# Attention keys of the second mixer: stored whole and split after the reload, with ScalarE and SyncE work moved around them

## The chip, the cores and the metric

The kernel runs on one core of a Trainium2 chip. The metric is the time of one execution in microseconds on the device. Engines are named as in the profile: PE is TensorE (PEld its weight loads), ACT is ScalarE, DVE is VectorE, POOL is GpSimd, SP is SyncE, which here does nothing but issue DMAs.

## The reference, cut to what matters

Two transformer blocks in a row work on 256 tokens of width 1024 in float32, and the second has 16 more rows of "meta tokens" in front, so 272 key rows. The second block's mixer projects its input and runs two attentions, a windowed one with grouped heads (16 query heads over 4 key heads) and a differential one (8 heads, each with two query and key parts):

```
q, k = rope(q), rope(k)
s_band = einsum(q, k_window) * scale; p = softmax([s_band, s_meta, sink])      # windowed
p = softmax(einsum(q, k) * scale + key_bias); a = p[0] - lam * p[1]; o = a @ v # differential
merged = 0.5 * (1 + tanh(..)) gates of both, @ w_out
```

## The kernel before, in words

**Products from two parts.** A float32 number is held as a high part in fp32r and a low part, `low = x - high`, also fp32r. ACT makes the high part (a copy that rounds), DVE or POOL the low part (a subtraction), and PE adds the products of the parts.

**Weights.** They come in blobs of 1 MB, one DMA each into a `raw` buffer (L748). ACT makes `whi` (L862), DVE makes `wlo` (L1859), and PE multiplies. In the second mixer three buffers take turns; `m2` counts its blobs from 0. A load waits until the blob three before it is split; a `whi` waits until the blob three before it is used up.

**Slots.** A blob is multiplied in two halves. After half `part` of blob `m2` PE runs `slot(q)` with `q = 2 * m2 + part`; ACT, DVE, and after the change POOL, have a loop over the same `q`, in which the order of their work is written out by hand, and no engine leaves its order. In the slots q = 22 to 53 PE makes the scores of one attention unit each, U = 0 to 31 (0 to 15 windowed, 16 to 31 differential). Unit U goes through: scores on PE in slot 22 + U (L1755), maximum on DVE and exponentials on ACT (L1165) in 23 + U, DVE's reciprocal (L2075) and for windowed units ACT's scaling (L1197) also in 23 + U, transposes on PE in slot 24 + U (L1689), values on PE in slot 25 + U.

**What the blobs hold.** Blobs 0 to 4 give keys, blobs `QUERIES` give queries, blobs `VALUES` give values. Key and query blobs are rotated: ACT (with DVE) moves the result from PSUM to `kraw`, SP's `swap_halves` copies it with swapped partition halves to `kswap` (two DMAs, L786 and L787), DVE multiplies both by the tables in `turn` and adds them into `kswap` (L2347 to L2349 for keys, L2337 to L2340 for queries). `kraw` and `kswap` have two buffers, by `m2 % 2`.

**Keys before.** `keys_high` (ACT, L1104) makes the high part in `knat`, POOL the low part (L1357), `store_keys` (SP, L794 to L798) writes both to DRAM as `key_parts`, 544 KB a blob. From there SP loads one chunk at a time to `kB`, two DMAs of 272 KB (L805): chunks 0 and 1 behind the loads of blobs 12 and 13, for the windowed units, and one for each two differential units.

**Queries.** `queries_high` (ACT, L1112) makes high parts twice, POOL the low part `ql` (L1364), SP moves it (L826).

**Values.** `values_out` (ACT, L1122) moves the values of a blob from PSUM to `kraw`, PE transposes them at the head of the slot in `VALUES_AT` (L1726), and `values_in` (ACT, L1138) brings them back in the next slot. PE waits in that slot for `values_out`.

## Time and profile before

| what | value |
| --- | --- |
| median of 3 runs | 876.76 us (876.65 to 877.49) |
| profiled execution | 876.87 us, of it 875.1 us span from first to last instruction |
| PE busy | 862.2 us, 99% of the span |
| PE weight load busy | 737.9 us, 84% |
| DVE, ACT, POOL busy | 629.0 (72%), 468.0 (53%), 73.7 (8%) |
| granted PE clock | 0.999 of full speed |

Time outside the span is 1.8 us. Slot 0 begins at about 396 us of the span. "Idle before" in a row names what ended the idle time.

### The profile page before, as it was taken

How to read it: one execution, taken by the hardware profiler on the slowest of the kernel's cores; microseconds unless marked ns; L12 is line 12 of the kernel's file. 1: busy time of each engine (PE TensorE's matmuls, PEld its weight loads, DVE VectorE, ACT ScalarE, POOL GpSimd, SP SyncE). 2: the span in 40 equal slices, each digit the busy share in tenths (PEclk: the TensorE clock that was granted, in tenths of full speed). 3: DMA queues.
4: the chain of work that ended last, by engine and by line, in shares of the span. 5: the costliest groups of instructions: out<-in, count | busy, mean ns of one | idle time of the engine just before them, and what ended most of it. 6: DMA issues, size and time to landing. Idle time of an engine off the chain costs nothing.

```text
span 875.1 us, 13099 instructions
## 1 busy us (share of the span) xinstructions
PE 862.2 (99%) x4820; PEld 737.9 (84%) x4820; DVE 629.0 (72%) x985; ACT 468.0 (53%) x756; POOL 73.7 (8%) x96
## 2 busy tenths in 40 slices
PE   8999999999999999999999999999999999999997
PEld 6887788888888888889889888788888888888886
DVE  5867677766876666668778887888766876666665
ACT  6546534434644444444566887676653654444443
POOL 1000000000200000002322010133300100000000
PEclk9999999999999999999999999999999999999999
DMA  9955344554565555352798443755474365455531
GB/s 331 400 212 192 116 169 149 192 188 149 186 241 191 192 192 192 144 192 86 259 274 288 136 157 117 246 192 172 169 269 173 122 225 190 177 198 188 189 143 48
DMA packets 31774, 167.21 MB, mean 191 GB/s; under 512 B 4128, under 2 KB 5920, under 8 KB 14320
## 3 DMA queue, kind: packets, MB, share of 16 engines
q1 hardware_dynamic: 28992, 159.17, 51.8%
q10 hardware_dynamic: 2736, 7.42, 2.4%
q8 instruction: 29, 0.48, 0.2%
q14 instruction: 17, 0.14, 0.0%
HBM read 157.02 MB, written 3.83 MB: 184 GB/s over the span
## 4 chain that ended last, share of the span: by engine, by line
PE 86%; DVE 6%; ACT 3%; DMA 1%; issue 1%; POOL 1%; SPq 0%; ACTq 0%; DVEq 0%
PE ps L522 16%; PE ps L524 16%; PE ps L523 16%; PE ps L688 8%; PE ps L673 8%; PE ps L692 4%; PE ps L669 4%; PE ps L701 2%; DVE wlo L1859 2%; ACT whi L862 1%; PE ps L557 1%; PE ps L1755 1%; DMA kswap<-kraw 1%; PE ps L703 1%; PE ps L1713 1%
## 5 line engine op out<-in xcount | busy, mean ns | idle before, releaser
L1859 DVE TENSOR_TENSOR wlo<-raw,whi 128x2048 fp32r<-128x2048 f32 x134 | 307.4, 2295 | 146.3 <-ACT whi L862 145.9
L862 ACT ACTIVATE whi<-raw 128x2048 fp32r<-128x2048 f32 x134 | 256.2, 1913 | 180.0 <-PE ps L524 109.0
L522 PE MATMUL ps<-whi,xT 128*128 128x512 f32 x192 | 76.8, 400 | 0.0
L524 PE MATMUL ps<-whi,xT 128*128 128x512 f32 x192 | 75.0, 391 | 0.0
L523 PE MATMUL ps<-wlo,xT 128*128 128x512 f32 x192 | 74.8, 390 | 0.0
L1326 POOL TENSOR_TENSOR stat<-stat,cst 128x1 f32<-128x1 f32 x10 | 11.9, 1200 | 490.0 <-DVE stat L1879 261.0
L522 PE MATMUL ps<-whi,fT_h 128*128 128x512 f32 x128 | 50.2, 392 | 0.0
L523 PE MATMUL ps<-wlo,fT_h 128*128 128x512 f32 x128 | 49.8, 389 | 0.0
L524 PE MATMUL ps<-whi,fT_l 128*128 128x512 f32 x128 | 49.8, 389 | 0.0
L522 PE MATMUL ps<-x_all,whi 128*128 128x272 f32 x160 | 46.5, 291 | 1.6 <-DVE wlo L1859 1.5
L523 PE MATMUL ps<-x_all,whi 128*128 128x272 f32 x160 | 46.1, 288 | 0.0
L524 PE MATMUL ps<-x_all,wlo 128*128 128x272 f32 x160 | 46.1, 288 | 0.0
L1165 ACT ACTIVATE sc<-sc,usoft 128x272 f32<-128x272 f32 x64 | 32.7, 512 | 22.7 <-DVE usoft L2067 18.7
L524 PEld LDWEIGHTS ps<-whi,xT 128*128 128x128 f32 x192 | 36.0, 188 | 7.8
L522 PEld LDWEIGHTS ps<-whi,xT 128*128 128x128 f32 x192 | 36.1, 188 | 7.4
L523 PEld LDWEIGHTS ps<-wlo,xT 128*128 128x128 f32 x192 | 36.1, 188 | 7.0
L673 PE MATMUL ps<-x_all,whi 128*128 128x512 f32 x176 | 42.0, 391 | 0.0
L688 PE MATMUL ps<-x_all,whi 128*128 128x512 f32 x160 | 38.0, 390 | 0.0
L522 PE MATMUL ps<-whi,x_all 128*128 128x512 f32 x96 | 38.0, 396 | 0.0
L524 PE MATMUL ps<-whi,x_all 128*128 128x512 f32 x96 | 37.7, 393 | 0.0
L673 PEld LDWEIGHTS ps<-x_all,whi 128*128 128x128 f32 x176 | 32.3, 188 | 6.3
L523 PE MATMUL ps<-wlo,x_all 128*128 128x512 f32 x96 | 37.6, 391 | 0.0
(349 smaller groups left out, 1886.9 us busy)
## 6 DMA issues: line engine op xcount, KB each, us to landing
raw<-weights SPq DMA_DIRECT2D x134, 1024.0 KB, 4.8
kB<-key_parts SPq DMA_DIRECT2D x20, 272.0 KB, 3.5
kswap<-kraw SPq DMA_DIRECT2D x26, 136.0 KB, 2.5
key_parts<-knat SPq DMA_DIRECT2D x4, 544.0 KB, 7.3
cst<-consts SPq DMA_DIRECT2D x1, 1371.0 KB, 13.3
raw<-weights SPq DMA_DIRECT2D x4, 256.0 KB, 5.1
raw<-weights SPq DMA_DIRECT2D x2, 512.0 KB, 6.7
gate_a<-gain_rows ACTq DMA_DIRECT2D x2, 512.0 KB, 7.9
```

The source lines that it names most:

```text
L522: pe.matmul(o, lh, rh, start=first, stop=False)
L523: pe.matmul(o, lh, rl, start=False, stop=False)
L524: return pe.matmul(o, ll, rh, start=False, stop=last)
L669: pe.matmul(ps[:, bank0 + j, 0:TOK], vl[:, k, j * P:(j + 1) * P], x[:, 0, k, :], start=k == 0, stop=False, skip_group_check=True)
L673: m = pe.matmul(ps[:, bank0 + j, :], vh[:, k, j * P:(j + 1) * P], x[:, :, k, :], start=False, stop=k == KC - 1, skip_group_check=True)
L688: pe.matmul(ps[:, bank0 + j, :], vh[:, k, j * P:(j + 1) * P], x[:, :, k, :], start=k == 0, stop=False)
L692: m = pe.matmul(ps[:, bank0 + j, 0:TOK], vl[:, k, j * P:(j + 1) * P], x[:, 0, k, :], start=False, stop=k == KC - 1)
L701: pe.matmul(ps[:, bank + j, :], vh[:, k, j * P:(j + 1) * P], x2[:, :, k, :], start=k == 0, stop=False)
L862: act.activation(whi[s][:], raw[s][:], ACT.Copy).then_inc(split_hi, 1)
L1165: ins = act.activation(scores(U, u), scores(U, u), ACT.Exp, bias=st[:, 2, u:u + 1], accum_out=st[:, 4, u:u + 1])
L1326: pool.tensor_tensor(st[:, 3:4], st[:, 2:3], c("neghalf")[:, 0:1], ALU.pow).then_inc(rstd_ok, 1)
L1859: dve.tensor_tensor(wlo[s][:], raw[s][:], whi[s][:], ALU.subtract).then_inc(split_lo, 1)
```

## The change

Keys are stored as they come from the rotation, unsplit (272 KB a blob), straight from `kswap`. A chunk is loaded back to a new buffer `ktwo` (two of them), and only then ACT makes its high part and POOL its low part in `kB`. That takes place in ten steps e = 0 to 9, in the slots of the new table `KEYS_AT`. `queries_high` moves from ahead of the exponentials to the end of its slot, the DMAs of the gate rows `gate_s` move from ACT to SP, and blob 11 now holds queries and blob 12 values (before the other way round).

```diff
-QUERIES = (6, 7, 9, 10, 12, 13, 15, 17)
+QUERIES = (6, 7, 9, 10, 11, 13, 15, 17)
-VALUES = (5, 8, 11, 14, 16)
+VALUES = (5, 8, 12, 14, 16)
-VALUES_AT = {12: 0, 18: 1, 24: 2, 30: 3, 34: 4}
+VALUES_AT = {12: 0, 18: 1, 26: 2, 30: 3, 34: 4}
+KEYS_AT = {17: 0, 19: 1, 32: 2, 38: 3, 40: 4, 42: 5, 44: 6, 46: 7, 48: 8, 50: 9}
+def stored(i):
+    return 16 * (i // 2 + 1) + (0 if i % 2 else 32)
...
@@ SP: swap_halves
-                if swaps_before(m2):
-                    sp.wait_ge(kt_ok, max(SWAPPED.index(m) for m in SWAPPED if m < m2 and m % 2 == b) + 1)
+                last = max((m for m in SWAPPED if m < m2 and m % 2 == b), default=None)
+                if last in QUERIES:
+                    sp.wait_ge(kt_ok, QUERIES.index(last) + 1)
+                elif last is not None:
+                    sp.wait_ge(kd_out[b], stored(last))
@@ SP: store_keys
-                sp.wait_ge(kt_ok, i + 1)
-                parts = knat[i % 2][:].bitcast(F32)
+                sp.wait_ge(rot_ok, i + 1)
+                v = kswap[i % 2]
                 if i:
-                    sp.dma_start(kd[i], parts).then_inc(kd_out[i % 2], 16)
+                    sp.dma_start(kd[i], v[:]).then_inc(kd_out[i % 2], 16)
@@ SP: load_keys, in the iterations 12 to 15 and 22 to 27 of the load loop
+                i, cc = (0, e) if e < 2 else (e // 2, e % 2)
+                if e == 0:
+                    sp.wait_ge(kd_out[0], stored(4))
+                    sp.wait_ge(kd_out[1], stored(3))
+                if e >= 2:
+                    sp.wait_ge(kb_lo, e - 1)
+                for u in range(2):
+                    v = kd[i, u::2, cc].unsqueeze(1).to_broadcast([DH, 2, KEYS])
+                    sp.dma_start(ktwo[e % 2][:, u, :], v).then_inc(ktwo_in[e % 2], 16)
...
+                if m == 22:
+                    sp.wait_ge(u_sc, S_UNITS)
+                    for t in range(NT):
+                        sp.dma_start(gate_s[:, t, :], grow[5].partition_broadcast(P)).then_inc(bias_in[2], 16)
@@ ACT
+            def keys_high(e):
+                act.wait_ge(ktwo_in[e % 2], 32 * (e // 2 + 1))
+                if e >= 2:
+                    act.wait_ge(u_sc, sets_read(e))
+                act.activation(kB[e % 2][:, :, 0, :], ktwo[e % 2][:], ACT.Copy).then_inc(kb_hi, 1)
...
-                if q in (4, 6, 8, 10, 12):
-                    keys_high(q // 2 - 2)
-                if q % 2 == 1 and (q - 5) // 2 in QUERIES:
-                    queries_high((q - 5) // 2)
...
-                if q == 38:
-                    act.wait_ge(u_sc, S_UNITS)
-                    bias_rows(2, gate_s)
+                if q % 2 == 1 and (q - 5) // 2 in QUERIES:
+                    queries_high((q - 5) // 2)
+                if q in KEYS_AT:
+                    keys_high(KEYS_AT[q])
@@ POOL, now in the same loop over q, in ACT's order
+            def keys_rest(e):
+                pool.wait_ge(kb_hi, e + 1)
+                pool.tensor_tensor(kB[e % 2][:, :, 1, :], ktwo[e % 2][:], kB[e % 2][:, :, 0, :],
+                                   ALU.subtract).then_inc(kb_lo, 1)
@@ PE
-                        pe.wait_ge(kb_in[key_slot(U)], keys_loaded(U))
+                        pe.wait_ge(kb_lo, key_set(U) + 1)
```

**First place.** ACT in the slots q = 16 to 20, before (L1112 is `queries_high`, L1122 `values_out`, L862 a `whi`, L1138 `values_in`):

```order
L862 ACTIVATE whi_56<-raw_55 128x2048
L1112 ACTIVATE qs_135<-kswap_119 128x512
L1112 ACTIVATE qs_136<-kswap_119 128x512
L1122 ACTIVATE kraw_117<-ps 128x544
L862 ACTIVATE whi_59<-raw_58 128x2048
L1134 ACTIVATE vb_meta<-ps 16x256
L1138 ACTIVATE vb<-ps,stat 128x256 x2
L1112 ACTIVATE qs_135<-kswap_120 128x512
```

and in the changed kernel (lines 5 higher; L1109 is the new `keys_high`):

```order
L867 ACTIVATE whi_56<-raw_55 128x2048
L1117 ACTIVATE qs_135<-kswap_119 128x512
L1117 ACTIVATE qs_136<-kswap_119 128x512
L1109 ACTIVATE kB_123<-ktwo_121 128x2x272
L1127 ACTIVATE kraw_117<-ps 128x544
L867 ACTIVATE whi_59<-raw_58 128x2048
L1139 ACTIVATE vb_meta<-ps 16x256
L1143 ACTIVATE vb<-ps,stat 128x256 x2
```

`keys_high(0)`, which waits for a DMA, now stands ahead of `values_out(1)`, the values of blob 8.

**Second place.** ACT in the slots q = 25 and 26, before (L1165 exponentials, L1176 and L1181 small copies, L1197 scaling, L1096 `queries_low`):

```order
L1138 ACTIVATE vb<-ps,stat 128x256 x2
L1112 ACTIVATE qs_135<-kswap_119 128x512
L1112 ACTIVATE qs_136<-kswap_119 128x512
L1165 ACTIVATE sc_142,usoft<-sc_142,usoft 128x272 x2
L1168 ACTIVATE usoft<-usoft 128x2
L1176 ACTIVATE pmT<-ps 48x128
L1181 ACTIVATE sT_h<-ps 128x128
L1197 ACTIVATE sc_142<-sc_142,usoft 128x272 x2
L1096 ACTIVATE kraw_117<-ps 128x2x256
```

and in the changed kernel:

```order
L1166 ACTIVATE sc_142,usoft<-sc_142,usoft 128x272 x2
L1169 ACTIVATE usoft<-usoft 128x2
L1177 ACTIVATE pmT<-ps 48x128
L1182 ACTIVATE sT_h<-ps 128x128
L1198 ACTIVATE sc_142<-sc_142,usoft 128x272 x2
L1117 ACTIVATE qs_135<-kswap_119 128x512
L1117 ACTIVATE qs_136<-kswap_119 128x512
L1127 ACTIVATE kraw_117<-ps 128x544
```

The last row, `values_out(2)`, now stands here, behind the scaling and behind `queries_high` of blob 10; before, it stood in slot 24, right behind the scaling of unit 0.

**Third place.** DVE in slot q = 24, before (L2337 to L2340 rotate the queries of blob 10, L2074 and L2075 end unit 1's row sums):

```order
L2065 TENSOR_TENSOR usoft<-usoft,negsink 128x2
L2337 TENSOR_TENSOR kraw_117<-kraw_117,turn 128x2x256
L2338 TENSOR_TENSOR kswap_119<-kswap_119,turn 128x2x256
L2340 TENSOR_TENSOR kswap_119<-kraw_117,kswap_119 128x2x256
L2074 TENSOR_TENSOR usoft<-usoft 128x2
L2075 RECIPROCAL usoft<-usoft 128x2
```

and in the changed kernel (12 lines higher):

```order
L2077 TENSOR_TENSOR usoft<-usoft,negsink 128x2
L2341 TENSOR_TENSOR kraw_118<-ps,kraw_118 128x2x256
L2349 TENSOR_TENSOR kraw_117<-kraw_117,turn 128x2x256
L2350 TENSOR_TENSOR kswap_119<-kswap_119,turn 128x2x256
L2352 TENSOR_TENSOR kswap_119<-kraw_117,kswap_119 128x2x256
L2086 TENSOR_TENSOR usoft<-usoft 128x2
L2087 RECIPROCAL usoft<-usoft 128x2
```

The first step of blob 11's queries, `queries_raw` (L2341), now stands ahead of the rotation; it waits for ACT's `queries_low` of the same slot.

## Rows read from the trace of the kernel before

**Rows 1.** Waits of PE over the whole span: us in total, times, longest:

```profile
PE ps L701 <- ACT vs L1138: 1.7, 1, 1.7
PE ps L522 <- DVE wlo L1859: 1.5, 1, 1.5
...
PE ps L1689 <- DVE sT_l L2407: 0.8, 1, 0.8
PE ps L1726 <- ACT kraw L1122: 0.6, 1, 0.6
```

**Rows 2.** Timeline of DVE in the key stage: start, us, what, idle before:

```profile
415.92 0.72 DVE L2349 TENSOR_TENSOR kswap<-kraw,kswap 128x544 f32<-128x544 f32 x1
...
423.78 0.73 DVE L2347 TENSOR_TENSOR kraw<-kraw,turn 128x544 f32<-128x544 f32 x1 [0.28 <-DMA kswap<-kraw]
424.42 1.90 DVE L2348 TENSOR_TENSOR kswap<-kswap,turn 128x544 f32<-128x544 f32 x1
...
437.59 0.72 DVE L2347 TENSOR_TENSOR kraw<-kraw,turn 128x544 f32<-128x544 f32 x1 [2.92 <-DMA kswap<-kraw]
...
439.63 2.29 DVE L1859 TENSOR_TENSOR wlo<-raw,whi 128x2048 fp32r<-128x2048 f32 x1
```

**Rows 3.** Timeline of POOL, the low part of key blob 1:

```profile
424.32 1.41 POOL L1357 TENSOR_TENSOR knat<-kswap,knat 128x544 fp32r<-128x544 f32 x1 [5.54 <-ACT knat L1104]
```

**Rows 4.** Timeline of SP, the DMA issues named in the text:

```profile
418.81 0.50 SPq L796 DMA_DIRECT2D key_parts<-knat  x1
...
441.94 0.33 SPq L748 DMA_DIRECT2D raw<-weights  x1
443.13 0.33 SPq L794 DMA_DIRECT2D key_parts<-knat  x1
...
452.76 1.58 SPq L805 DMA_DIRECT2D kB<-key_parts  x2
```

**Rows 5.** Issue to landing of the three weight loads (L748) issued from 405 to 423:

```profile
DMA to landing us min/median/max: 4.8/5.0/5.1
```

**Rows 6.** The same of the three stores of key blob 0 (418 to 421):

```profile
DMA to landing us min/median/max: 2.1/2.4/2.6
```

**Rows 7.** The same of L786, the first half of swaps, from 403 to 422:

```profile
DMA to landing us min/median/max: 2.2/2.3/2.3
```

**Rows 8.** The same of the two key loads (L805) issued at 452.8 and 453.8:

```profile
DMA to landing us min/median/max: 6.8/7.8/8.7
```

**Rows 9.** Timeline of PE: blobs 7 and 9, value transposes, unit transposes:

```profile
443.64 2.08 PE L701 MATMUL ps<-x_all,whi 128*128 128x512 f32 x8 [1.70 <-ACT vs L1138]
...
455.32 2.01 PE L701 MATMUL ps<-x_all,whi 128*128 128x512 f32 x8
...
458.13 0.38 PE L1726 MATMUL ps<-cst,kraw 128*128 128x128 f32 x2
...
481.72 0.60 PE L1689 MATMUL ps<-cst,sc 128*128 128x128 f32 x4
...
486.58 0.66 PE L1689 MATMUL ps<-cst,sc 128*128 128x128 f32 x4
```

**Rows 10.** Timeline of ACT: value copies, scalings and query parts named in the text:

```profile
457.14 0.60 ACT L1122 ACTIVATE kraw<-ps 128x544 f32<-128x544 f32 x1
...
475.69 0.94 ACT L1197 ACTIVATE sc<-sc,usoft 128x272 f32<-128x272 f32 x2 [2.36 <-DVE usoft L2075]
...
479.11 0.94 ACT L1197 ACTIVATE sc<-sc,usoft 128x272 f32<-128x272 f32 x2 [0.20 <-DVE usoft L2075]
...
482.74 1.14 ACT L1112 ACTIVATE qs<-kswap 128x512 fp32r<-128x512 f32 x2
...
485.59 0.94 ACT L1197 ACTIVATE sc<-sc,usoft 128x272 f32<-128x272 f32 x2 [0.30 <-DVE usoft L2075]
```

**Rows 11.** Timeline of DVE, the low part of blob 14, in slot 25:

```profile
481.89 2.29 DVE L1859 TENSOR_TENSOR wlo<-raw,whi 128x2048 fp32r<-128x2048 f32 x1 [1.11 <-ACT whi L862]
```

**Rows 12.** Timeline of ACT in slot 38, behind the issue of the gate rows:

```profile
551.36 1.92 ACT L862 ACTIVATE whi<-raw 128x2048 fp32r<-128x2048 f32 x1 [0.54 <-issue]
```

More of the change, by code:

```diff
@@ L143, in query_of, with key_set, sets_read @@
     return U // S_UNITS * 4 + cc // 2
-def key_slot(U):
+def key_set(U):
     cc, _ = unit_place(U)
-    return cc // 4 if U < S_UNITS else cc % 2
-def keys_loaded(U):
-    cc, _ = unit_place(U)
-    return 32 if U < S_UNITS else 32 + 32 * (cc // 2 + 1)
+    return cc // 4 if U < S_UNITS else 2 + cc
+def sets_read(e):
+    return 0 if e < 2 else 8 if e == 2 else 2 * e + 10
+def stored(i):
+    return 16 * (i // 2 + 1) + (0 if i % 2 else 32)
 def slot_of(n):
@@ L299, in build @@
         kswap = [new("kswap0", [P, 2, KEYS]), new("kswap1", [P, 2, KEYS])]
-        keys_at = top[0]
-        knat = [new("knat0", [P, 2, 2, KEYS], F32R), new("knat1", [P, 2, 2, KEYS], F32R)]
-        top[0] = keys_at
-        kB = [new("kB0", [P, 4, KEYS]), new("kB1", [P, 4, KEYS])]
+        ktwo = [new("ktwo0", [P, 2, KEYS]), new("ktwo1", [P, 2, KEYS])]
+        kB = [new("kB0", [P, 2, 2, KEYS], F32R), new("kB1", [P, 2, 2, KEYS], F32R)]
         vs_meta = new("vs_meta", [P, S_KV * DH])
         o_junk = new("o_junk", [P, P])
-        rrow2 = at("rrow2", [P, TOK], F32, top[0])
-        ql = [new("ql0", [P, 2, TOK], F32R)]
+        rrow2 = new("rrow2", [P, TOK])
         assert top[0] <= 3 * BLOB
@@ L435, in build @@
         kd_out = [sem("kd_out0"), sem("kd_out1")]
-        kb_in = [sem("kb_in0"), sem("kb_in1")]
+        ktwo_in = [sem("ktwo_in0"), sem("ktwo_in1")]
+        kb_hi = sem("kb_hi")
+        kb_lo = sem("kb_lo")
         q_in = [sem(f"q_in{j}") for j in range(len(QUERIES))]
@@ L1096, in queries_low @@
                 act.activation(kraw[b][:, :, 0:TOK], ps[:, bank:bank + 2, TOK:2 * TOK], ACT.Copy).then_inc(ql_ok, 1)
-            def keys_high(i):
-                act.wait_ge(rot_ok, i + 1)
-                if i >= 2:
-                    act.wait_ge(kd_out[i % 2], 16 * (i // 2) + (0 if i % 2 else 32))
-                act.activation(knat[i % 2][:, :, 0], kswap[i % 2][:], ACT.Copy).then_inc(rot_hi, 1)
+            def keys_high(e):
[3 more added lines that the diff above has]
+                act.activation(kB[e % 2][:, :, 0, :], ktwo[e % 2][:], ACT.Copy).then_inc(kb_hi, 1)
             def queries_high(m2):
                 i = QUERIES.index(m2)
-                act.wait_ge(rot_ok, 5 + i + 1)
+                act.wait_ge(rot_ok, SWAPPED.index(m2) + 1)
                 j = QUERY_PLACE[i]
@@ L1353, in _, with queries_rest @@
             pool.memset(pmT[:], 0.0).then_inc(zero2, 1)
-            for i in range(5):
+            def queries_rest(m2):
+                i = QUERIES.index(m2)
+                j = QUERY_PLACE[i]
                 pool.wait_ge(rot_hi, i + 1)
-                pool.tensor_tensor(knat[i % 2][:, :, 1], kswap[i % 2][:], knat[i % 2][:, :, 0],
-                                   ALU.subtract).then_inc(kt_ok, 1)
-            for i, m2 in enumerate(QUERIES):
-                pool.wait_ge(rot_hi, 5 + i + 1)
                 if i >= 2:
                     pool.wait_ge(q_in[QUERY_PLACE[i - 2]], 32)
-                j = QUERY_PLACE[i]
                 pool.tensor_tensor(ql[i % 2][:], kswap[m2 % 2][:, :, 0:TOK],
@@ L1366, in _ @@
                                    ALU.subtract).then_inc(kt_ok, 1)
-            for U in range(S_UNITS, UNITS):
-                pool.wait_ge(d_o, U - S_UNITS + 1)
-                st = ostat[:, U % 3]
-                link(pool, "pool", rsqrt(st[:, 2:3], st[:, 1:2], st[:, 0:1], 1.0 / P))
-                pool.tensor_scalar(o_tok[U % 3][:], o_tok[U % 3][:], st[:, 2:3], None, ALU.mult).then_inc(d_n, 1)
+            def keys_rest(e):
+                pool.wait_ge(kb_hi, e + 1)
+                pool.tensor_tensor(kB[e % 2][:, :, 1, :], ktwo[e % 2][:], kB[e % 2][:, :, 0, :],
+                                   ALU.subtract).then_inc(kb_lo, 1)
+            for q in range(2 * OUT2):
+                if q % 2 == 1 and (q - 5) // 2 in QUERIES:
+                    queries_rest((q - 5) // 2)
+                if q in KEYS_AT:
+                    keys_rest(KEYS_AT[q])
+                U = q - U0 - 3
+                if S_UNITS <= U < UNITS:
+                    pool.wait_ge(d_o, U - S_UNITS + 1)
+                    st = ostat[:, U % 3]
+                    link(pool, "pool", rsqrt(st[:, 2:3], st[:, 1:2], st[:, 0:1], 1.0 / P))
+                    pool.tensor_scalar(o_tok[U % 3][:], o_tok[U % 3][:], st[:, 2:3], None, ALU.mult).then_inc(d_n, 1)
             for t in range(NT):
@@ L1755, in slot @@
                             m = pe.matmul(ps[:, 4 + u, 0:KEYS], qT[u][:, cc, t * P:(t + 1) * P],
-                                          kT[:, 2 * u + v, 0:KEYS].bitcast(F32R), start=v == 0, stop=v == 1)
+                                          kT[:, u, v, :], start=v == 0, stop=v == 1)
                     m.then_inc(u_sc, 1)
```

40 lines of the change are left out of this document (14 added, 26 removed).

## The prediction

> **What bounds the kernel now.** I read the page first: PE is busy 99% of the span at its full clock, so apart from its start and end the kernel is as long as PE's own work plus PE's waits. The changed kernel gives PE the same products and transposes. What the change can win or lose is therefore PE's waits in the second mixer, and the list of PE's waits shows all that there is to win [rows 1]: 1.5 us for the low part of blob 5, 1.7 for `vs`, the values of blob 5, 0.6 for `values_out(3)`, 0.8 for `sT_l` in slot 40; 4.6 us in all. What there is to lose has no such limit. So I followed the timelines of DVE, SP and ACT through slots 4 to 40 and asked at each wait of PE what is late next. Times below are on the clock of the profiled execution (span 875.1 us, with 1.8 us around it 876.9; the median of the runs, 876.76, is 0.1 lower).
>
> **Key stage, slots 4 to 15.** Removed: five ACT copies, five POOL subtractions, half of the bytes of the stores. Added: a swap into `kswap` must now wait until the store that reads it has *landed*, where before it waited for POOL.
>
> Rotation of key blob 0 ends at 415.92 + 0.72 = 416.6 [rows 2]. Its stores went out at 418.8, behind ACT and POOL [rows 4]; now at 416.7. Three issues take some 1.2 us and the last lands 2.1 later [rows 6], at 420.0; the swap's second half leaves 0.6 behind the first and lands after another 2.4 (the first half took 2.3 [rows 7]): 423.0, against 423.75 before, when DVE woke up [rows 2]. The rotation then takes 2.0 (437.59 to 439.63), without the 1.2 us which one of its steps lost, 1.90 for 0.72, while POOL worked from 424.32 to 425.73 [rows 2, 3]. With 2.3 for the low part, blob 5 is ready at 427.35, when PE comes: the wait of 1.5 goes.
>
> For blobs 3 and 4 the new wait costs what the removed work gives. Their stores stand behind a weight load of 1 MB, which lands 4.8 to 5.1 after its issue [rows 5]. For blob 4: weight load out at 428.3, landed at 433.3, the store 0.7 behind it (a guess: half of the 1.4 that the transfer of the 544 KB appears to take), swap out at 434.1 and 434.7, landed at 437.0, against 437.6 before [rows 2]. 2.0 + 2.3 later, at 441.4 to 441.8, blob 7 is ready, against 441.9. `vs` is ready before that, since `keys_high(4)` no longer stands in front of it on ACT. PE begins blob 7 at about 441.65 instead of 443.64 [rows 9]: **-2.0 us** so far, with a short wait left.
>
> **Slot 18, `keys_high(0)` ahead of `values_out(1)`.** This is the first place of the order. PE does 455.32 - 443.64 = 11.7 us for blobs 7 and 8 and 2.8 for the first half of blob 9 [rows 9], so it stands at the transposes of blob 8's values at 458.13 - 2.0 = 456.1. It needs `values_out(1)`, which before ran at 457.14 [rows 10], and now waits on ACT behind `keys_high(0)`, thus for the landing T of the first key chunk. T from SP's order: weight load 10 can leave when blob 7 is split, 441.65 (before 441.94 [rows 4]); it lands 5.0 later and the store of key blob 4 0.7 behind it, 447.3. Only then may the swap of blob 6 leave (new wait), and SP with it; 1.2 for its two issues, weight load 11 at 448.6, the swap of blob 7, weight load 12 at 450.7, the key chunk at 451.3 and 451.9 (before from 452.76 [rows 4]). Ahead of the chunk stand two weight loads and a swap. From below: load 11 lands 5.0 after 448.6, and of those 5.0 some 2.3 are there for a small DMA as well [rows 7], so load 12 takes 2.7 more, swap and chunk some 0.5 each: 457.3. From above: the chunk lands as late after its issue as before, 6.8 and 8.7 [rows 8], 458.1 and 460.6. I take T = 458.5. The copy and `values_out(1)` take 0.6 each [rows 10]: PE goes on at 459.8 against 458.13, **+1.65** on before, which swallows the 2.0 (a wait of 3.7 us). Bounds -0.1 to +3.6 (T from 456.7 to 460.5); no wait at all needs T below 454.8. The scores of slot 22 wait for `kb_lo` of this chunk, ready at 461, and are no problem.
>
> **Slots 24 to 26, second and third place.** From here on I use before's times and count only what differs, since all follows PE. Blob 11 is queries, so DVE in slot 24 has `queries_raw(11)` ahead of the rotation of blob 10. It waits for `queries_low(11)` on ACT, which waits behind `queries_high(9)`, now behind the scaling of unit 0. That began at 475.69 and took 0.9 [rows 10]; DVE's sums in front of it had met POOL's low part of blob 9, which now comes later, so it begins some 1.1 earlier (what POOL cost DVE in slot 6) and ends at 475.5: 475.5 + 1.1 + 0.6 = 477.1. `queries_raw` 0.7, rotation 2.0 with 0.2 lost to POOL's low part of blob 9, sums 0.3: 480.3; scaling 0.9 [rows 10]: 481.3. PE comes to the transposes of unit 1 at 480.9 (before 481.72 [rows 9], 0.4 less for the shorter blob, 0.6 less for the value transposes that went to slot 26, 0.2 more for the values blob now in hand). So it starts them at 481.35: a wait of 0.5.
>
> Behind the scaling ACT makes the high part of blob 14 (1.9), 483.1; DVE the low part (2.3), 485.45 (before at 481.89 [rows 11]); sums and scaling of unit 2 end at 486.75 (before 485.59 + 0.94 = 486.5 [rows 10], and PE took it at 486.58 [rows 9]). Now `queries_high(10)` follows (1.14 [rows 10]) and then `values_out(2)` (0.6): 488.3. PE is at the transposes of blob 12's values at 486.2, waits 2.1, and starts unit 2 after 0.57 more (the six value transposes) at 488.9 instead of 486.58: **+2.3**. Bounds: +0.9 if the sums of unit 1 and of unit 2 come 0.7 earlier each; +3.1 if POOL's subtraction (1.4 [rows 3]) holds up DVE's `queries_raw` too.
>
> One row bears on that last bound. In slot 6 the DVE step from `kswap` and `turn`, both in SBUF, ran 1.90 and ended 0.6 after POOL, as if it had begun when POOL ended [rows 2, 3]. The Trainium skill (SBUF — State Buffer, "Who interferes with whom") says that DVE with two inputs in SBUF and a POOL operation that reads SBUF exclude each other for a whole instruction, whoever comes first. The trace agrees, 1.90 for 0.72. By that rule `queries_raw`, which has one input in PSUM, isn't held, as I assumed above; were it held, the sum would be 0.8 higher.
>
> **Later slots.** `values_out(3)` in slot 30 loses what stood in front of it (`queries_high(12)` in slot 29 is gone): PE's 0.6 goes, **-0.65** with its start. In slot 38 the gate rows' issue cost ACT 0.54 [rows 12]; in its place stands `keys_high(3)`, 0.6: nothing. In slot 39 `queries_high(17)` comes later and POOL's part falls on DVE's sums, scaling and `sT_l`: the wait of 0.8 in slot 40 stays, **+0.2** (bounds -0.8 to +0.5). The seven key steps in slots 38 to 50 cost ACT 0.6 each and may each hold DVE 1.1. I cost them at nothing: PE waits nowhere after slot 40 [rows 1], and ACT (53% busy) and DVE (72%) run ahead of it there. Without that cover each would cost up to 1.7, 12 us in all. The loads of the chunks leave two slots or more before their step; SP's wait for the last windowed unit (slot 37) stands before weight load 23, needed in slot 42.
>
> **Sum.** -2.0 + 3.65 (slot 18, that is +1.65 net) + 2.3 - 0.65 + 0.2 = **+3.5 us**: 880.3 us on the median. Its own range by the bounds is 877.5 to 883.5.
>
> **Rivals.** *The chunk is in time* (chance 0.10). The chunk's DMAs are issued behind two weight loads but may overtake them: before, the first of the two key loads took 6.8 and the second 8.7 though issued one after the other [rows 8], so they are not in step. Both must land, by 454.8, 3 us after the issue. Against it: the second took 8.7. Then slot 18 costs nothing and the sum is -2.0 + 2.3 - 0.65 + 0.2 = -0.15: 876.6. The Trainium skill (DMA: Bandwidth & Descriptors, "Queues, rings and completion order") says that the DMAs of one issuing engine need not complete in order, which would make this more likely than a strict queue does; the trace shows it for halves of pairs alone.
>
> *Only slot 18 costs* (0.14): ACT is a microsecond or two earlier in slot 26 than I have it, PE finds `values_out(2)` ready; -2.0 + 3.65 - 0.65 + 0.2 = +1.2: 878.0.
>
> *ACT never holds PE* (0.12), the other side: ACT is far enough ahead at both value copies. The place is ACT's order ahead of L1127, the price of it is both waits; it decides when `values_out(1)` is done by 456.1 and `values_out(2)` by 486.2. Then the relief of the key stage stays, slots 30 and 40 give their waits back as well: -2.0 - 0.65 - 0.8 = -3.5: 873.3. For it: the key traffic is halved, and a weight load that stands alone takes 5.0, not more.
>
> *Traffic gets worse* (0.04): small stores and swaps each waiting for the one before, T at 464: 885.
>
> *As forecast* 0.60.
>
> **Numbers.** About 0.2% (1.75 us) is what a measurement of this kernel can tell from no change, so "same" is 875.0 to 878.5. Faster: all of the third rival and a part of the first, 0.16. Same: most of the first, half of the second and the low edge of the forecast, 0.18. Slower 0.66. The range 876.0 to 883.6 holds the forecast, the first two rivals and leaves out the third.
>
> **What would show it.** Key stage: no wait of PE for blob 5, blob 7 begun near 441.7, swaps issued right after a store's landing. Slot 18: PE waits 2 to 5 us for `kraw` of ACT (L1127), and ACT before that for the DMA `ktwo`. Slot 26: PE waits about 2 us for `kraw` again. Slot 30: no wait. Slots 41 to 53: none. The prediction is wrong above all if ACT's wait for `ktwo` in slot 17 is under 1 us, or if a key step of the later slots holds DVE long enough to stop PE.

## Result and the profile after

The changed kernel took **884.4 us** (median of 6 runs, 883.4 to 886.7), the kernel before 876.7 on the same chip: a ratio of 1.0089, interval 1.0076 to 1.0103. Run once more beside other experiments it took 884.5 (1.0102, 1.0084 to 1.0119). The forecast was 880.3, slower, with a range up to 883.6: the sign and the places were right, the sum was 4.1 us short.

One profiled execution, that of the run with the shorter delay below (c2), ran at a granted clock of 0.65 throughout and took 1222.8 us; it is used nowhere.

The first profiled execution took 886.7, 2.3 above the median. The rows here are those of a second one, of 884.5 (span 882.7 against 875.1 before), unless the text says "first". PE's waits over the whole span, in the columns of [rows 1]:

```profile
PE ps L1738 <- ACT kraw L1127: 7.2, 2, 5.4
PE ps L708 <- DVE wlo L1871: 2.3, 2, 1.2
...
PE ps L1753 <- issue: 0.3, 1, 0.3
PE ps L529 <- DVE wlo L1871: 0.2, 1, 0.2
```

Of the four waits of [rows 1] three are gone, that of blob 5 nearly; in their place stand two waits for the landing of a store in the key stage (blobs 6 and 7) and two for a value copy (slots 18 and 26). The timeline of PE there:

```profile
442.16 1.21 PE L708 MATMUL ps<-x_all,whi 128*128 128x512 f32 x4 [1.19 <-DVE wlo L1871]
...
462.21 0.69 PE L1738 MATMUL ps<-cst,kraw 128*128 128x128 f32 x2 [5.36 <-ACT kraw L1127]
...
463.40 3.11 PE L708 MATMUL ps<-x_all,whi 128*128 128x512 f32 x8
...
493.52 0.44 PE L1738 MATMUL ps<-cst,kraw 128*128 128x128 f32 x2 [1.86 <-ACT kraw L1127]
```

The first row answers to 443.64 in [rows 9], the second to 458.13: PE comes 1.5 us earlier into blob 7, and 4.1 later to the end of its wait in slot 18. The timeline of ACT says why, in both slots:

```profile
460.99 0.66 ACT L1109 ACTIVATE kB<-ktwo 128x544 fp32r<-128x544 f32 x1 [6.66 <-DMA ktwo<-key_parts]
461.55 0.60 ACT L1127 ACTIVATE kraw<-ps 128x544 f32<-128x544 f32 x1
...
490.99 0.94 ACT L1198 ACTIVATE sc<-sc,usoft 128x272 f32<-128x272 f32 x2 [1.21 <-DVE usoft L2087]
491.83 1.13 ACT L1117 ACTIVATE qs<-kswap 128x512 fp32r<-128x512 f32 x2
492.87 0.60 ACT L1127 ACTIVATE kraw<-ps 128x544 f32<-128x544 f32 x1
```

In slot 17 ACT waited 6.7 us for the DMA of `keys_high(0)` (L1109), with `values_out(1)` (L1127) behind it. In slot 26 `values_out(2)` stands behind the scaling and `queries_high(10)`: PE stood there from 491.66, the scaling ended 0.3 later, and the copies of both took the rest of the wait. Issues of SP, and the time from issue to landing of the two loads of chunk 0:

```profile
442.51 0.43 SPq L804 DMA_DIRECT2D key_parts<-kswap  x1
448.18 0.47 SPq L796 DMA_DIRECT2D kswap<-kraw  x1
...
452.01 1.59 SPq L820 DMA_DIRECT2D ktwo<-key_parts  x2
```

```profile
DMA to landing us min/median/max: 7.0/7.5/7.9
```

The swap of blob 6 left when the store had landed. The two loads of the chunk, issued at 452.0 and 453.0, landed at 459.0 and 461.0.

**What I had not looked for** is in the third PE row. The same eight matmuls, right behind the value transposes, took 3.11 us here and 2.08 before:

```profile
458.71 2.08 PE L701 MATMUL ps<-x_all,whi 128*128 128x512 f32 x8
```

Windows of the first profiled execution over two stretches, one from the end of the wait in slot 18 on, one behind the wait in slot 26 (us, busy time and count of PE, PEld, DVE, ACT, POOL, then PE's granted clock, DMA share, GB/s):

```profile
460.69:467.52 6.83, 5.64 (x19) 4.70 (x20) 2.29 (x1) 5.49 (x9) 3.15 (x3) 0.50 0.25 92
494.83:498.24 3.41, 3.41 (x22) 2.69 (x20) 2.34 (x5) 0.83 (x6) 0.45 (x1) 0.50 0.39 154
```

TensorE ran at 1.2 GHz instead of 2.4 in both. In the second execution the stretch began at 458.8, inside the wait, and ended at 465.6, and none followed slot 26. Before, the clock was at 2.4 GHz from 9.5 us of the span to its last 2 us.

The price of a stretch can be read behind slot 26. Nine profiles (these two and seven of the experiments) have that wait. From its end to the scores of slot 27 PE took 7.0 us in the three in which no stretch follows, and 8.5 to 8.6 us in the six in which one does.

Where the 7.6 us between the two profiled executions (875.1 and 882.7) lie, read from the start of PE's score matmuls, which every slot from 22 to 53 has once:

| place | forecast | measured |
|---|---|---|
| key stage, start of blob 7 | -2.0 | -1.5 |
| slot 18, value transposes 458.13 to 462.21 | +3.65 | +5.6 |
| slots 18 to 22, clock at half | 0 | +1.4 |
| slots 24 to 26 | +2.3 | +2.1 |
| slot 30 | -0.65 | -0.8 |
| slot 40 | +0.2 | -1.0 |
| slots 44 to 53 | 0 | +1.8 |
| sum | +3.5 | +7.6 |

The last place, slots 44 to 53, in the scores of slots 44 and 53, before and after:

```profile
576.82 0.75 PE L1755 MATMUL ps<-kB,qd 128*128 128x272 f32 x4
...
616.51 0.75 PE L1755 MATMUL ps<-kB,qd 128*128 128x272 f32 x4
```

```profile
582.67 0.75 PE L1767 MATMUL ps<-kB,qd 128*128 128x272 f32 x4
...
624.13 0.75 PE L1767 MATMUL ps<-kB,qd 128*128 128x272 f32 x4
```

39.7 us became 41.5. I call this the late stretch below.

### The profile page after: what moved, and what is told of

The parts are those of the page before. It is cut to its first block, busy times and chain, and to the rows that moved or that the text cites. A ratio compares the mean times of both kernels' runs of the same rounds, so it can differ in the third digit from the quotient of the medians.

```text
span 884.9 us, 13113 instructions
## 1 busy us (share of the span) xinstructions
PE 866.8 (98%) x4820; PEld 740.4 (84%) x4820; DVE 625.8 (71%) x985; ACT 468.9 (53%) x761; POOL 78.4 (9%) x101
## 4 chain that ended last, share of the span: by engine, by line
PE 92%; DMA 3%; DVE 2%; ACT 1%; SPq 1%; issue 1%; DVEq 0%; ACTq 0%
PE ps L529 18%; PE ps L531 17%; PE ps L530 17%; PE ps L695 8%; PE ps L680 7%; PE ps L699 4%; PE ps L676 4%; PE ps L1767 2%; PE ps L708 2%; DMA key_parts<-kswap 1%; PE ps L564 1%; PE ps L1701 1%; PE ps L710 1%; DMA ktwo<-key_parts 1%; PE ps L1725 1%; PE ps L1720 1%
## 5 line engine op out<-in xcount | busy, mean ns | idle before, releaser
L1328 POOL TENSOR_TENSOR stat<-stat,cst 128x1 f32<-128x1 f32 x10 | 9.9, 1003 | 489.4 <-DVE stat L1891 260.4
```

## Experiments

The kernels ran in sets on different chips, each beside the kernel before, whose median there was 875.8 to 877.0 us. The ratio in brackets is to that median, with its interval. So times of different sets can't be told apart below 1 us; there the profiles have to decide.

**The chunk one slot later.**

```
-KEYS_AT = {17: 0, 19: 1, ...
+KEYS_AT = {18: 0, 20: 1, ...
```

> The changed kernel with the high parts of key chunks 0 and 1 made in slots 18 and 20 instead of 17 and 19, so that `values_out(1)` stands ahead of the wait for the first chunk. Theory A (the wait of 5.4 us in slot 18 costs itself and, through TensorE's granted clock at 0.5 for 6.8 us behind it, some 2 us more): PE finds `values_out(1)` ready, no stretch at 0.5 begins near 460, and the time falls by 6.5 to 7.5 us to about 877.4. Theory B (the wait alone counts, the time at the lower clock is hidden under what PE would have waited for anyway): 884.4 - 5.4 = 879.0. Theory C (ACT and SP are held by the landing of the chunk wherever the step stands, so the wait comes back one or two slots later at a weight blob): 882 or more.

Measured: 883.7 us (ratio to before 1.0074, 1.0062 to 1.0087). C was right. `values_out(1)` was in time, and the wait stood one step further on ACT, at `values_in(1)`, which frees the PSUM pair (timeline of PE, then of ACT):

```profile
463.53 2.90 PE L708 MATMUL ps<-x_all,whi 128*128 128x512 f32 x6 [3.90 <-ACT vb L1143]
```

```profile
459.95 0.66 ACT L1109 ACTIVATE kB<-ktwo 128x544 fp32r<-128x544 f32 x1 [5.91 <-DMA ktwo<-key_parts]
460.51 1.89 ACT L867 ACTIVATE whi<-raw 128x2048 fp32r<-128x2048 f32 x1
462.31 0.36 ACT L1139 ACTIVATE vb_meta<-ps 16x256 f32<-16x256 f32 x1
462.58 0.80 ACT L1143 ACTIVATE vb<-ps,stat 128x256 f32<-128x256 f32 x2
```

From the landing of the chunk to PE's release it is now 3.6 us instead of 1.2, so that the wait of 5.4 us became only 3.9, although PE came 2.8 later to it and the chunk landed 1.0 earlier. The median fell by 0.7, which is within the two intervals.

**The chunk behind all of it.**

```
-KEYS_AT = {17: 0, 19: 1, ...
+KEYS_AT = {20: 0, 21: 1, ...
```

> The changed kernel with the high parts of key chunks 0 and 1 in slots 20 and 21, behind both `values_out(1)` (slot 18) and `values_in(1)` (slot 19). Theory A (the chunk's landing near 460.6 costs only because values of blob 8 stand behind it on ACT; with slot 18 alone passed by, the wait moved from 5.4 us at L1127 to 3.9 us at L1143): both waits gone, and the time at a granted clock of 0.5 that begins behind them too: 884.4 - 5.4 - 1.5 to 2 = 877.2. Theory B (ACT has no place before slot 22 at which the chunk can be taken without holding PE; the wait moves to a weight blob or to the scores of slot 22): 881 or more.

Measured: 877.3 (1.0016, 1.0003 to 1.0028), 7.1 below the changed kernel, or 6.4 by the two ratios. A was right: the wait was 5.4, and the rest went with it. The chunk landed no earlier (461.3); now nothing stood behind it on ACT that PE was waiting for. Of PE's waits for ACT one was left, slot 26:

```profile
PE ps L1738 <- ACT kraw L1127: 1.9, 1, 1.9
```

**The chunk's DMA ahead of the others.** The loads of chunk 0 are issued behind the store of blob 4, ahead of the swap of blob 6; ACT's place stays slot 17.

```
                 if 6 <= m < 11:
                     store_keys(m - 6)
+                if m == 10:
+                    load_keys(0)
-                if 12 <= m < 16:
+                if 13 <= m < 16:
```

> The changed kernel with one thing moved: SP issues the loads of key chunk 0 right behind the store of key blob 4, when this has landed, and ahead of the swap of blob 6, instead of behind two weight loads and the swaps of blobs 6 and 7. ACT's step stays in slot 17. Theory A (the landing at 460.6 is late because the chunk was issued at 451.7 and 452.7 behind two weight loads, and the landing, not ACT's place alone, makes the wait): issued at 448 to 449, ahead of the loads issued later, it lands by 453 to 455, ACT does not wait into slot 18, and the time is that of key steps in slots 20 and 21, 877.3. Theory B (the chunk's load takes 7 to 8 us whenever it is issued, since weight loads issued behind it share the queues): landing near 456.5, a wait of PE of about 1.5 us in slot 18, 878.5 to 880. Theory C (the swap of blob 6, later by 1.2 us, is what becomes late): a wait of 1 us or more for the queries of blob 6 or for `values_out(1)` behind them.

Measured: 881.0 (1.0049, 1.0033 to 1.0064). The landing was as A said and far below B's 7 to 8 us:

```profile
DMA to landing us min/median/max: 2.5/2.7/2.8
```

The same two loads of 136 KB take 2.5 and 2.8 us with no weight load on its way, and 7.0 and 7.9 behind two weight loads of 1 MB and a swap. PE did not wait in slot 18. But the gain was half. What SP issued behind the chunk was later (the next weight load by 0.7, its landing by 1.8), and PE waited in four new places besides slot 26 (L1740):

```profile
PE ps L1740 <- ACT kraw L1129: 1.9, 1, 1.9
PE ps L1703 <- ACT sc L1200: 1.1, 1, 1.1
PE ps L1769 <- DVE usoft L2079: 0.5, 1, 0.5
PE ps L708 <- ACT vb L1145: 0.3, 1, 0.3
...
PE ps L708 <- DVE kraw L2343: 0.3, 1, 0.3
```

**Queries ahead of the exponentials again.** `queries_high` goes back to where it stood before, in all its slots.

```
+                if q % 2 == 1 and (q - 5) // 2 in QUERIES:
+                    queries_high((q - 5) // 2)
                 if q == 14:
...
-                if q % 2 == 1 and (q - 5) // 2 in QUERIES:
-                    queries_high((q - 5) // 2)
                 if q in KEYS_AT:
```

> The changed kernel with `queries_high` back ahead of the exponentials of its slot, and nothing else undone. Theory A (in slot 26 `values_out(2)` comes late because `queries_high(10)` stands between the scaling of unit 2 and it; the 1.85 us of PE's wait also bring a stretch of 3.4 us at a granted clock of 0.5, which costs about 1.6 more): both go, 884.4 - 3.4 = 881.0. Theory B (the wait alone): 882.6. Theory C (the wait of slot 26 comes from the scaling of unit 2 and the high part of the weight blob, and `queries_high` in front of the exponentials costs the units what it gives the values): 884.4 or more.

Measured: 885.1 (1.0099, 1.0084 to 1.0113). A and B are refuted, C was right: the wait of slot 26 stayed at 1.9 and a wait of 0.6 for `sT_l` came back in slot 40. The 1.1 us of `queries_high(10)` in front of `values_out(2)` were gone, but the scaling ended at 492.4, and PE stood at the value transposes from 491.1. The scaling was late because its row sum on DVE was. DVE's step here, and in the changed kernel:

```profile
490.02 1.25 DVE L2086 TENSOR_TENSOR usoft<-usoft 128x2 f32<-128x2 f32 x1
```

```profile
490.60 0.15 DVE L2086 TENSOR_TENSOR usoft<-usoft 128x2 f32<-128x2 f32 x1
```

With `queries_high(10)` earlier, POOL's low part of the same queries ran beside DVE's sums, from 488.90 to 491.25; in the changed kernel it began at 493.04, behind them. So the place of `queries_high(10)` costs about 1.1 us on either side of the scaling: as a copy behind it, or by POOL ahead of it.

**Blobs 11 and 12 as before.**

```
-QUERIES = (6, 7, 9, 10, 11, 13, 15, 17)
+QUERIES = (6, 7, 9, 10, 12, 13, 15, 17)
-VALUES_AT = {12: 0, 18: 1, 26: 2, 30: 3, 34: 4}
+VALUES_AT = {12: 0, 18: 1, 24: 2, 30: 3, 34: 4}
```

(`VALUES` and `TAKERS` go back with them.)

> The changed kernel with blobs 11 and 12 as before (11 values, 12 queries, `values_out(2)` in slot 24), all else as changed. Theory A (the order of the blobs costs PE its 1.85 us in slot 26, because DVE has the raw queries of blob 11 to make in slot 24 and ACT's scaling of unit 2 comes late; it gives back 0.65 in slot 30 and 1.0 in slot 40): 884.4 - 1.85 + 1.65 = 884.2, or 883 with a share of the clock. Theory B (`queries_high` behind the exponentials costs the 1.85 in whatever blob order): the wait stands in slot 24 or 26 again and slots 30 and 40 get their waits back, 886.

Measured: 883.3 (1.0079, 1.0062 to 1.0097). No wait in slot 24 or 26, none in slots 30 and 40 either. The order of the blobs, with the slot that it gives to `values_out(2)`, is the cause in slot 26, and undoing it gives nothing back elsewhere. The median is 1.1 us lower, which is within the intervals; between the scores of slots 22 and 30 PE took 38.4 us instead of 40.5 in the profiled executions. Together with the edit before (next run, of the same set as e5) it is clear of noise:

> Both edits: key chunks 0 and 1 in slots 20 and 21, blobs 11 and 12 as before. Theory A: the sum of the two single edits, 877.2 - 0.2 = 877.0, with what the late slots lose (1.8 us) still in it. Theory B (they are two covers of one lateness of ACT and DVE, so that the second edit gives nothing or less than alone): 877.2 to 879.

Measured: **875.4** (0.9990, 0.9981 to 0.9998): 1.9 below e5, which is the wait of slot 26, and 9 below the changed kernel. The granted clock is 1.0 up to the last 2 us, and these are PE's waits from 340 us on:

```profile
PE ps L708 <- DVE wlo L1871: 2.6, 2, 1.4
PE ps L1753 <- issue: 0.4, 1, 0.4
```

**Is the lower clock the wait's doing?** The kernel before, with copies of the unit matrix on ACT ahead of `values_out(1)` (the edit in short):

```
                 if i == 1:
+                    for o in (sT_h, qd[0], qd[1]):
+                        act.activation(o, unit matrix, ACT.Copy)
```

> The kernel before, with three copies of the unit matrix over 2048 columns (1.8 us each) put into ACT ahead of `values_out(1)` in slot 18; they write where nothing stands yet and change no result. PE had 0.4 us of margin there, so it should wait 5.4 - 0.4 = 5.0 us. Theory A (a wait of such length is itself followed by a stretch at a granted clock of 0.5, whoever causes it): such a stretch of some 3.4 to 6.8 us begins within 1 us behind the wait, and the time is 876 + 5.0 + 1.5 to 2 = 882.5 to 883. Theory B (the lower clock in the changed kernel comes from something else in it): clock 1.0 throughout, and 881.0 at most.

Measured: 882.3 (1.0068, 1.0054 to 1.0081); its profiled execution is the fastest of the six, 879.8, and the others took 881.9 to 883.2. The wait was 3.3 us in it, not 5.0: the copies began at 454.1, as soon as blob 8 was through, 2.8 us before PE stood at the transposes. The timeline of PE:

```profile
460.14 0.44 PE L1730 MATMUL ps<-cst,kraw 128*128 128x128 f32 x2 [3.31 <-ACT kraw L1126]
...
460.86 3.57 PE L701 MATMUL ps<-x_all,whi 128*128 128x512 f32 x8
```

The clock was 0.5 from 460.7 to 464.1, and eight matmuls took 3.57 instead of 2.08 (at 458.71): 1.5 us on top of the wait. B is refuted; the old kernel shows the same when PE is made to wait. With a shorter delay:

> As the run before, with one copy over 2048 columns and one over 512, 2.3 us: a wait of PE of 1.9 us in slot 18, as long as that in slot 26 of the changed kernel. In four profiles with a wait of 1.9 us in slot 26, three had a stretch of 3.4 us at 0.5 behind it and two had none; the waits of 1.1 to 1.7 us in the key stage never had one. Theory A: 876 + 1.9 = 877.9 without a stretch, 879.3 with one, so that single runs spread by 1.4 us. Theory B (a wait of under 2 us costs itself only): 877.9 and no stretch.

Measured: 876.3 (0.9998, 0.9987 to 1.0008), the median of executions of 875.4 to 878.0. The time doesn't show the delay; a delay of 2.3 us fits into the 2.8 us of room that the longer one had, but no usable profile shows that it did. So this run says nothing on the clock behind a short wait. (The count in its expectation is wrong: of the seven profiles with a wait of 1.9 us in slot 26 taken up to then, five had a stretch behind it and two had none.)

The changed kernel once more:

> The changed kernel once more, unchanged. Over its six times so far those with a mean clock of 0.998 were 883.4 and 883.6 us, with 0.996 884.1 and 884.7, with 0.994 884.7 and 886.7. Theory A (each stretch of 3.4 us at 0.5 costs about 1 us and comes and goes between executions): the same steps again, 1.0 to 1.3 us per 0.002 of mean clock, median 884.4. Theory B (the spread has another cause): no relation between clock and time.

Measured: 884.5. All eleven executions of the changed kernel, by the mean clock of the span:

| mean clock | us |
|---|---|
| 0.997 to 0.998 | 883.1, 883.4, 883.6 |
| 0.996 | 883.7, 884.1, 884.5, 884.7 |
| 0.993 to 0.994 | 884.7, 885.9, 886.2, 886.7 |

The means are 883.4, 884.3 and 885.9. The time follows the clock as A says, 0.9 and 1.6 us a step. That is a relation, not an intervention, but the eight matmuls at either level, and the 7.0 against 8.5 to 8.6 us behind slot 26, give such a price too.

**The late stretch.** Orders of the key steps and cuts of their halves, with a table of all at the end. First, POOL's normalisation ahead of `keys_rest`:

```
-                if q in KEYS_AT:
-                    keys_rest(KEYS_AT[q])
                 U = q - U0 - 3
                 if S_UNITS <= U < UNITS:
                     ...
+                if q in KEYS_AT:
+                    keys_rest(KEYS_AT[q])
```

> The changed kernel with POOL's normalisation of `o_tok` ahead of `keys_rest` in a slot that has both (slots 42 to 50). Theory A (PE loses some 1.8 us in slots 44 to 51 because `keys_rest` of 1.4 us stands ahead of the normalisation that PE's transpose of `o_tok` needs): 884.4 - 1.8 = 882.6. Theory B (the normalisation is late because DVE holds it up while it runs, 2.1 to 2.6 us instead of 0.6, whatever stands ahead of it): no change, 884.4.

Measured: 886.0 (1.0110, 1.0095 to 1.0124), 1.6 more on the median, which the intervals don't tell from nothing, but the late stretch took 42.4 instead of 41.5; neither theory had that. Together with the two first edits:

> The three edits together: key chunks 0 and 1 in slots 18 and 20, `queries_high` ahead of the exponentials, the normalisation ahead of `keys_rest`. Theory A (each loss is local and the clock's share goes with its wait): 884.4 - 7.0 - 3.4 - 1.8 = 872.2, faster than the kernel before by 0.5%. Theory B (waits alone, clock and order on POOL worth nothing): 884.4 - 5.4 - 1.85 = 877.1, as before. Theory C (a wait that goes in slot 18 comes back in part further on): 878 or more.

Measured: 887.9 (1.0119, 1.0104 to 1.0133). C, and worse. Of three repairs drawn from the trace alone none is measurably better than the changed kernel by itself (-0.7, +0.7 and +1.6 on the medians), and the three together are 3.5 slower. `keys_high` at the head of the slot for q from 38 on:

> The changed kernel with the key steps of slots 38 to 50 (ACT's copy) at the head of their slot, ahead of the exponentials, so that POOL's subtraction is through before the unit's `o_tok` comes. Theory A (PE's loss of 1.8 us in slots 42 to 53 comes from the collision of POOL's two steps with the low part of the weight blob on DVE, and an earlier `keys_rest` takes it away): 882.6. With the normalisation first the loss had grown by about 1 us instead, since the subtraction then ran into DVE's next steps. Theory B (any subtraction of 1.4 us on POOL in these slots holds DVE for as long, wherever it stands): 884.4, or more if the exponentials come late by 0.6.

Measured: 889.2 (1.0138, 1.0121 to 1.0155). The late stretch gained 0.3, but PE waited 2.1 us for `sT_l` in slot 40, and a third stretch at clock 0.5, of 3.4 us, began 0.9 behind that wait.

Then the halves of the step, cut to 16 of 272 columns on the kernel of 875.4:

> Key chunks 0 and 1 in slots 20 and 21 and the blobs as before, and POOL's subtraction for chunks 4 to 9 over 16 of 272 columns only, so that the low part of these keys is left out for the rest (what remains there is that of an earlier chunk). Theory A (the 1.85 us that slots 44 to 53 lose is POOL's 1.4 us per key step, which pushes the normalisation of `o_tok` into the low part of the weight blob): 875.4 - 1.7 = 873.7. Theory B (it is ACT's copy of 0.6 us in these slots that makes the unit's exponentials late): 875.4.

Measured: 875.1 (0.9986, 0.9976 to 0.9996). A is refuted: with most of POOL's subtraction gone the late stretch is as long, 41.4.

> Key chunks 0 and 1 in slots 20 and 21, the blobs as before, and for chunks 4 to 9 both ACT's copy and POOL's subtraction over 16 of 272 columns only: the split of the other columns is left out for the rest. With the subtraction alone cut it was 875.1, and the late slots took as long as before the cut. Theory A (ACT's copy of 0.64 makes the loss): copy of 0.2 us, the loss falls to a third or less, 875.2 - 1.2 to 1.8 = 873.6. Theory B (the loss is in neither, but in the loads of the chunks or in where PE stands): 875.1.

Measured: 873.7 (0.9972, 0.9963 to 0.9981), late stretch 39.8. A was right for ACT's copy on top of the subtraction; the copy cut alone was not run, so whether the subtraction would cost anything by itself in these slots isn't shown. The timeline of ACT and of DVE in slot 44, before:

```profile
577.76 0.34 ACT L1204 ACTIVATE dT_h<-ps,subgain 128x128 fp32r<-128x128 f32 x1
578.01 1.90 ACT L862 ACTIVATE whi<-raw 128x2048 fp32r<-128x2048 f32 x1
```

```profile
579.24 0.28 DVE L2067 TENSOR_SCALAR usoft<-usoft 128x2 f32<-128x2 f32 x1
579.94 2.29 DVE L1859 TENSOR_TENSOR wlo<-raw,whi 128x2048 fp32r<-128x2048 f32 x1 [0.43 <-ACT whi L862]
```

and in the changed kernel, with POOL last:

```profile
584.18 0.64 ACT L1109 ACTIVATE kB<-ktwo 128x544 fp32r<-128x544 f32 x1
584.73 1.90 ACT L867 ACTIVATE whi<-raw 128x2048 fp32r<-128x2048 f32 x1
```

```profile
585.61 0.69 DVE L2079 TENSOR_SCALAR usoft<-usoft 128x2 f32<-128x2 f32 x1
586.66 2.30 DVE L1871 TENSOR_TENSOR wlo<-raw,whi 128x2048 fp32r<-128x2048 f32 x1 [0.36 <-ACT whi L867]
```

```profile
584.91 1.36 POOL L1371 TENSOR_TENSOR kB<-ktwo,kB 128x544 fp32r<-128x544 f32 x1 [2.88 <-ACT kB L1109]
...
587.30 2.14 POOL L1384 TENSOR_SCALAR o_tok<-o_tok,ostat 128x128 f32<-128x128 f32 x1
```

`whi` starts 1.2 us behind the scores before (576.82) and 2.1 after (582.67); DVE's `wlo` is 0.9 later behind it, and the copies that PE needs in the next slot stand behind `wlo`; none of PE's waits there is longer than 0.3. ACT is idle for 1.6 us and more in the odd slots, but not in front of `whi`.

So the steps into the odd slots, where ACT has no weight blob, with POOL's normalisation first in this run and the ones after it:

```
-... 40: 4, 42: 5, 44: 6, 46: 7, 48: 8, 50: 9}
+... 40: 4, 41: 5, 43: 6, 45: 7, 47: 8, 49: 9}
```

> Key chunks 0 and 1 in slots 20 and 21 and the blobs as before (875.4 us), and in addition the steps of key chunks 5 to 9 in slots 41, 43, 45, 47, 49 instead of 42 to 50, POOL's normalisation of `o_tok` ahead of `keys_rest`. Theory A (the late slots lose 1.85 us because in even slots ACT's copy of 0.64 stands ahead of the high part of the weight blob, and so DVE's low part and the sums and `puT` behind it are late; in odd slots ACT has no weight blob and is idle for 1.6 to 2.7 us): slots 44 to 53 take 39.7 us again, 875.4 - 1.5 to 1.8 = 873.7. Theory B (any key step in these slots costs PE its 0.3 to 0.4 us, as did the steps at the head of the slot and with the normalisation first): 875.4.

Measured: 875.3 (0.9992, 0.9983 to 1.0001), late stretch 41.2: B. And with POOL's half cut there:

> The kernel with the late key steps in odd slots (875.3 us), and POOL's subtraction for chunks 4 to 9 over 16 of 272 columns only; the low part of the other columns is left out. Theory A (in odd slots ACT has room for the copy, and what is left of the loss is POOL's 1.36 us, during which DVE's small step for the maxima took 0.56 instead of 0.17 and ACT's next exponentials came late): slots 44 to 53 take 39.8 us, 875.3 - 1.4 = 873.9. Theory B (ACT's copy costs there as well): 41.2 us and 875.3.

Measured: 873.6 (0.9961, 0.9948 to 0.9975), late stretch 39.7. So in even slots the step costs by ACT's copy and in odd ones by POOL's subtraction. (By the ratios of the two sets the gain is 2.7 instead of 1.7; the profiles have 1.5.) Last, in even slots but behind `whi`:

> Key chunks 0 and 1 in slots 20 and 21, the blobs as before, the late key steps in their even slots but on ACT behind the high part of the weight blob, and on POOL behind the normalisation. Theory A (the place ahead of the weight blob's high part is all that costs): high part 1.2 us behind the scores again instead of 2.1, 873.7. Theory B (POOL's subtraction now stands right behind DVE's low part and holds DVE's next step, and the normalisation of the odd slot behind it): as with the steps ahead, 875.2 to 876.

Measured: 877.8 (1.0008, 0.9999 to 1.0017): the mechanism of B, at a higher price. POOL's subtraction took 2.9 us, beside `wlo` and then ahead of DVE's next step, which took 1.13 instead of 0.22 with `puT` behind it.

The first four rows are of the kernel before and the changed one, the others of e7:

| key steps of the late slots | late stretch, us |
|---|---|
| none (before) | 39.7 |
| even, as changed | 41.5 |
| even, normalisation first (e3) | 42.4 |
| even, head of slot (e8) | 41.2 |
| even, as changed (e7) | 41.5 |
| even, subtraction cut (c4) | 41.4 |
| even, both cut (d2) | 39.8 |
| odd (d1) | 41.2 |
| odd, subtraction cut (f1) | 39.7 |
| even, behind `whi` (f2) | 43.6 |

**The gate rows back on ACT**, on the kernel with the odd slots:

> The first kernel of this set with the gate rows' two loads back on ACT in slot 38, ahead of `queries_high` and the key step. Theory A (on either queue they are hidden): within 0.3 us of that kernel, 873.7. Theory B (ACT is tight around slot 38 to 40, where `sT_l` was 0.8 late before the change, and 0.54 us more of issue bring a wait of PE in slot 40): 0.5 to 1 us more.

Measured: 876.0 (1.0000, 0.9991 to 1.0009), 0.7 more in the same set, and a wait of PE of 1.1 for `sT_l` in slot 40: B. Timelines of POOL and DVE around slot 39, with the rows on ACT:

```profile
552.92 1.29 POOL L1363 TENSOR_TENSOR ql<-kswap,qd 128x512 fp32r<-128x512 f32 x1 [2.81 <-ACT qd L1113]
```

```profile
552.91 1.31 DVE L2089 SCALAR_TENSOR_TENSOR usoft<-usoft,neglam 128x1 f32<-128x1 f32 x1
```

and with the rows on SyncE:

```profile
553.27 1.59 POOL L1364 TENSOR_TENSOR ql<-kswap,qd 128x512 fp32r<-128x512 f32 x1 [3.12 <-ACT qd L1117]
```

```profile
552.95 0.22 DVE L2090 SCALAR_TENSOR_TENSOR usoft<-usoft,neglam 128x1 f32<-128x1 f32 x1
```

A DVE step on one number per partition takes 1.31 us when POOL's subtraction of the queries of blob 17 begins with it, and 0.22 when that begins 0.3 later. That is the wait of slot 40: before, this step took 1.06 at 555.72; with the queries first (e2), 1.05; in the changed kernel 0.22. The Trainium skill (SBUF — State Buffer, "Who interferes with whom") says that issue order, not the shape of the operation, decides who blocks. The trace agrees in the second pair, where the DVE step was through when POOL began. In the first the two starts lie 0.01 us apart, too close to say which came first; DVE's step ended with POOL's, at 554.2.

## Why the prediction was wrong in size

**Right.** The sign; both places and their chains, by name; the key stage's new wait for a store's landing (each of the swaps left 0.06 to 0.07 us behind a landing); slot 30 (-0.65 against -0.8); slots 24 to 26 (+2.3 against +2.1), where the chain through `wlo`, the sums, the scaling, `queries_high(10)` and `values_out(2)` ran as written; only the wait of 0.5 at unit 1 did not show. The blob order is the cause (e6).

**Mis-sized: "I take T = 458.5".** The chunk landed at 460.6 and 461.0. It was issued 0.7 to 1.1 later than in my chain, since blob 7 began at 442.16, not 441.65, with a wait of 1.2 where I had "a short wait", and the stores of 272 KB took 5.6 us and more behind a weight load. And it took 7.0 and 7.9 us, which lies within [rows 8] (6.8 and 8.7), my bound from above; I had gone part of the way towards a sum of what is left of other transfers. Of the two bounds one was a measured load of keys in the same place behind weight loads, though of twice the bytes, the other a construction. The wait was 5.4 for 3.7, and slot 18 cost 5.6 for 3.65. c3 shows that the loads in front make the 7 us. The rival in which the chunk is in time was right in kind alone: its first load landed at 459.0, 1.2 before the weight load issued ahead of it, its second at 461.0. The Trainium skill (DMA: Bandwidth & Descriptors, "Queues, rings and completion order") lets a later DMA complete first; the trace agrees, by 1.2 us.

**Failed: "apart from its start and end the kernel is as long as PE's own work plus PE's waits".** A wait of 5.4 us was followed by half clock on PE's own work: +1.4 up to slot 22 in the execution shown, and in the first 2.4 there and 1.5 more behind slot 26. e5, which takes the wait away and leaves the chunk's time, gave 7.1; c1 did it to the old kernel. This term alone would have brought the forecast to 881.7; with the wait at its measured size as well, 883.4.

**Failed: "I cost them at nothing".** I had argued from busy shares and from PE not waiting there, and looked for a stall of DVE by POOL. What costs is the place on ACT, ahead of `whi`: 1.8 us (c4, d2). I had even put the full price at up to 1.7 a step "without that cover"; it was 0.35 for each of the five steps from slot 42 on, and no single wait was longer than 0.3, so the list of PE's waits hardly shows it.

**Failed, to the good: "the wait of 0.8 in slot 40 stays".** It went, for 0.3 us between two starts, and two parts of the change each decide it: the gate rows, "nothing" in my sum, are worth 0.7 (d4), and with the queries ahead of the exponentials a wait of 0.6 is back (e2). This gain of 1.2 on the forecast hides part of the misses: without it the sum would have been 5.3 short. The places of the key stage and of slot 30 were within 0.5.

The bounds were added up wrongly too: one by one they give 876.1 to 883.3, not 877.5 to 883.5. It changes nothing, since the range on record was wider.

What stays open: why a wait of 1.9 us in slot 26 was followed by a stretch at 0.5 in six of nine profiles and by none in the other three.

The change without the two placements that made PE wait (e7) is 875.4, within 0.2% of the kernel before; no variant that computes everything was measurably faster by more. The split per chunk has room for some 1.5 us more (f1, which leaves out most of the low parts of the late chunks, 873.6), which no order tried here gives.

## What to carry to other kernels

A step that waits for a DMA goes behind everything that the bounding engine still needs from that queue, not one step behind: moving it past the first consumer only moved the wait (e1), moving it past both gave 6.4 to 7.1 us (e5). Where a bound of a transfer's time is a row of a like transfer behind like loads, take it. Price a copy added to an engine by what stands directly behind it there (here the weight blob's high part), never by that engine's busy share. Then count a long wait of TensorE dearer than its length.
